# Expert weights in pairs of contraction steps: rows of 22 and 24 KB, and two double ring slots in place of four

## The reference, cut to what matters

```python
affinity = softmax(h @ w_r)                       # 256 tokens, 16 experts
gate, idx = top_k(swapaxes(affinity, 1, 2), 32)   # each expert takes its 32 best tokens
xs = h[idx]                                       # 16 x 32 x 1024
hid = silu(xs @ w_g) * (xs @ w_u)                 # w_g, w_u: 16 x 1024 x 2816
ye = (hid @ w_d) * gate                           # w_d: 16 x 2816 x 1024
out = segment_sum(ye, idx)                        # back to 256 tokens
```

## Time and profile before

| | us |
|---|---|
| runs | 2527.23, 2523.57, 2525.76 |
| median | 2525.76 |
| span of the profiled execution | 2528.1 |
| PE busy | 1933.1 (76%) |
| DVE, ACT, POOL busy | 610.9, 533.0, 585.5 |
| share of the DMA queue of SP, of 16 engines | 74.8% |

### The profile page before, as it was taken

The page is one execution under the profiler, slowest core; times in us unless marked ns, Lnnn a source line. Parts: engine busy times, 40 slices in busy tenths (PEclk is TensorE's granted clock), DMA queues, the critical chain, the costliest instruction groups (busy, mean ns, idle before and its releaser), DMA issues.

```text
span 2528.1 us, 34453 instructions
## 1 busy us (share of the span) xinstructions
PE 1933.1 (76%) x14760; PEld 1173.2 (46%) x14760; DVE 610.9 (24%) x854; ACT 533.0 (21%) x847; POOL 585.5 (23%) x290
## 2 busy tenths in 40 slices
PE   5999887667766666667666676667998989897886
PEld 3786652221121211221112112216888989786776
DVE  4006630000000000000000000014238982235244
ACT  3331221000000000000000000004645434553552
POOL 1435300000000000000000000004626866563562
PEclk7999886665566656665666655667998999997897
DMA  8757489999999999999999999991543546342330
GB/s 338 258 186 288 148 309 400 423 421 426 425 426 425 425 426 426 425 425 426 426 425 426 425 426 425 425 413 62 167 134 125 175 150 194 124 133 84 123 128 17
DMA packets 157966, 760.54 MB, mean 301 GB/s; under 512 B 9751, under 2 KB 101655, under 8 KB 104120
## 3 DMA queue, kind: packets, MB, share of 16 engines
q1 hardware_dynamic: 154216, 754.07, 74.8%
q10 hardware_dynamic: 3664, 5.24, 0.6%
HBM read 756.13 MB, written 3.14 MB: 300 GB/s over the span
## 4 chain that ended last, share of the span: by engine, by line
DMA 44%; PE 40%; DVE 10%; issue 2%; ACT 2%; POOL 1%; SPq 0%; DVEq 0%; ACTq 0%; POOLq 0%
DMA ring<-in_w_exp_down 16%; PE ps L559 15%; DMA ring<-in_w_exp_up 14%; DMA ring<-in_w_exp_gate 13%; PE ps L793 7%; PE ps L553 3%; PE ps L914 2%; PE ps L806 2%; DVE arena L1565 2%; PE ps L513 2%; DVE ff_parts L1566 2%; PE ps L585 2%; DVE ff_parts L1567 1%; PE ps L896 1%; PE ps L679 1%
## 5 line engine op out<-in xcount | busy, mean ns | idle before, releaser
L793 PE MATMUL ps<-ring,arena 128*32 128x352 f32 x4096 | 625.2, 757 | 239.8 <-DMA ring<-in_w_exp_gate 135.5
L1630 POOL TENSOR_TENSOR ring_lo<-ring,w_hi 128x1024 fp32r<-128x1024 f32 x220 | 531.2, 2427 | 588.2 <-ACT w_hi L957 587.9
L559 PE MATMUL ps<-x_parts,w_hi 128*128 128x256 f32 x2688 | 537.5, 296 | 50.5 <-DVE x_parts L1266 40.1
L559 PEld LDWEIGHTS ps<-x_parts,w_hi 128*128 128x128 f32 x2688 | 444.4, 198 | 79.2 <-issue 48.1
L793 PEld LDWEIGHTS ps<-ring,arena 128*32 128x32 f32 x4096 | 147.0, 153 | 704.6 <-DMA ring<-in_w_exp_gate 258.8
L559 PE MATMUL ps<-x_parts,ring_lo 128*128 128x256 f32 x1344 | 391.5, 291 | 0.0
L806 PE MATMUL ps<-ring,arena 128*32 128x256 f32 x2816 | 235.3, 489 | 178.3 <-DMA ring<-in_w_exp_down 131.8
L559 PEld LDWEIGHTS ps<-x_parts,ring_lo 128*128 128x128 f32 x1344 | 267.8, 199 | 0.2 <-issue 0.2
L806 PEld LDWEIGHTS ps<-ring,arena 128*32 128x32 f32 x2816 | 98.8, 135 | 323.1 <-DMA ring<-in_w_exp_down 185.0
L957 ACT ACTIVATE w_hi<-ring 128x1024 fp32r<-128x1024 f32 x220 | 229.8, 1053 | 89.6 <-PE ps L914 50.3
L1477 DVE TENSOR_TENSOR arena<-arena,ps 128x704 f32<-128x704 f32 x16 | 14.2, 887 | 827.8 <-PE ps L793 827.8
(11 more groups left out here) (200 smaller groups left out, 1655.0 us busy)
## 6 DMA issues: line engine op xcount, KB each, us to landing
ring<-in_w_exp_gate SPq DMA_DIRECT2D x128, 1408.0 KB, 10.7
ring<-in_w_exp_up SPq DMA_DIRECT2D x128, 1408.0 KB, 10.9
ring<-in_w_exp_down SPq DMA_DIRECT2D x112, 1536.0 KB, 11.5
ring<-in_w_ada SPq DMA_DIRECT2D x48, 1536.0 KB, 8.7
ring<-in_w_in SPq DMA_DIRECT2D x30, 1536.0 KB, 7.2
ring<-in_w_ff SPq DMA_DIRECT2D x18, 1536.0 KB, 7.1
ring<-in_w_in SPq DMA_DIRECT2D x16, 1024.0 KB, 5.5
ring<-in_w_out SPq DMA_DIRECT2D x8, 1536.0 KB, 7.3
```

What stands on the lines that cost most here:

```text
L559: m = pe.matmul(ps[:, bank, 0:T], w, a, start=(k == 0 and j == 0), stop=(k == KD - 1 and j == 2))
L793: m = pe.matmul(ps[32 * j:32 * j + 32, 2 * (k // 8) + i, 0:FJ // 2], XCUR[:, k % 8, :], ring[:, s, at:at + FJ // 2], start=(k % 8 == 0), s ...
L1630: pool.tensor_tensor(slot(c["u"], KD, c["w"], of=ring_lo)[:, :, at], slot(c["u"], KD, c["w"])[:, :, at], w_hi[:, s % HI, :, :].bitcast(F32 ...
```

## The change

Two contraction steps are loaded together. The four slots are seen as two of 24 KB per partition (`ring_pairs`), with semaphores of their own, `pair_ready` and `pair_used`. An expert has 12 pairs: 4 of gate, 4 of up, 4 of down. A pair waits until the pair that held its slot before is used.

For gate and up, partition p now holds features 8 p to 8 p + 7, so that a pair is one row of 22 KB per partition, the rows 88 KB apart. To match, block c of XS takes every eighth feature: HTOK is read with a step of 8 floats. A pair of down is a row of 24 KB, the last one 16 KB. SP's loop over the experts is written out, the waits of ACT, DVE and POOL count pairs, and POOL's first copy of XCUR stands ahead of its loop. The number of matmuls and their order on PE stay as they are.

```diff
-EXP_UNITS = 24
+EXP_RING = 2
+EXP_PAIRS = 12
+DOWN_C = 6
...
+        pair_ready = [S(f"pair_ready{i}") for i in range(EXP_RING)]
...
+        ring_pairs = ring.rearrange("p (a b) n -> p a (b n)", a=EXP_RING)
...
             def load(u, dst, src):
-                if u >= RING:
+                if exp0 <= u < exp0 + RING:
+                    last = EXPERTS * EXP_PAIRS - EXP_RING + u % RING // (RING // EXP_RING)
+                    sp.wait_ge(S("pair_used"), last + 1)
+                elif u >= RING:
                     sp.wait_ge(S("unit_used"), u - RING + 1)
                 sp.dma_start(dst, src).then_inc(w_ready[u % RING], 16)
...
-            gate = inp["w_exp_gate"].rearrange("a e (k p) f -> (a e) p k f", p=P)
-            up = inp["w_exp_up"].rearrange("a e (k p) f -> (a e) p k f", p=P)
+            gate = inp["w_exp_gate"].rearrange("a e (p k) f -> (a e) p (k f)", p=P)
+            up = inp["w_exp_up"].rearrange("a e (p k) f -> (a e) p (k f)", p=P)
             down = inp["w_exp_down"].rearrange("a e (p c) d -> (a e) p (c d)", p=P)
-            with sp.Fori(0, EXPERTS) as e:
-                for k in range(EXP_UNITS):
-                    sp.wait_ge(S("unit_used"), e * EXP_UNITS + (exp0 + k - RING + 1))
-                    s = (exp0 + k) % RING
-                    if k < 16:
-                        src = (gate if k < 8 else up)[e, :, k % 8, :]
-                        dst = ring[:, s, 0:F_EXP]
+            for e in range(EXPERTS):
+                for q in range(EXP_PAIRS):
+                    n = e * EXP_PAIRS + q
+                    i = n % EXP_RING
+                    if n < EXP_RING:
+                        sp.wait_ge(S("unit_used"),
+                                   1 + max(u for u in range(exp0) if u % RING // (RING // EXP_RING) == i))
                     else:
-                        c0 = 3 * (k - 16)
-                        c1 = min(c0 + 3, FC)
+                        sp.wait_ge(S("pair_used"), n - EXP_RING + 1)
+                    if q < 8:
+                        src = (gate if q < 4 else up)[e, :, 2 * (q % 4) * F_EXP:2 * (q % 4 + 1) * F_EXP]
+                        dst = ring_pairs[:, i, 0:2 * F_EXP]
+                    else:
+                        c0 = DOWN_C * (q - 8)
+                        c1 = min(c0 + DOWN_C, FC)
                         src = down[e, :, c0 * D:c1 * D]
-                        dst = ring[:, s, 0:(c1 - c0) * D]
-                    sp.dma_start(dst, src).then_inc(w_ready[s], 16)
+                        dst = ring_pairs[:, i, 0:(c1 - c0) * D]
+                    sp.dma_start(dst, src).then_inc(pair_ready[i], 16)
...
-                    m = pe.matmul(ps[:, c % 4, :], HTOK[:, t, P * c:P * c + P], SEL[:, t, :, :],
+                    m = pe.matmul(ps[:, c % 4, :], HTOK[:, t, :].rearrange("p (q k) -> p k q", k=KD)[:, c, :],
+                                  SEL[:, t, :, :],
                                   start=(t == 0), stop=(t == NT - 1))
...
+                for q in range(8):
+                    pe.wait_ge(pair_ready[q % EXP_RING], e * (16 * EXP_PAIRS // EXP_RING) + 16 * (q // EXP_RING + 1))
+                    for k in (0, 1):
+                        x = XCUR[:, 2 * (q % 4) + k, :]
+                        for i in range(2):
+                            for j in range(CG):
+                                at = F_EXP * k + FJ * j + FJ // 2 * i
+                                m = pe.matmul(ps[32 * j:32 * j + 32, 2 * (q // 4) + i, 0:FJ // 2], x,
+                                              ring_pairs[:, q % EXP_RING, at:at + FJ // 2],
+                                              start=(q % 4 == 0 and k == 0), stop=(q % 4 == 3 and k == 1),
+                                              skip_group_check=True)
+                    count(m, "pair_used")
...
+                for q in range(8, EXP_PAIRS):
+                    pe.wait_ge(pair_ready[q % EXP_RING], e * (16 * EXP_PAIRS // EXP_RING) + 16 * (q // EXP_RING + 1))
+                    c0 = DOWN_C * (q - 8)
+                    for c in range(c0, min(c0 + DOWN_C, FC)):
...
-            with pool.Fori(0, EXPERTS) as e:
-                pool.wait_ge(S("unit_used"), e * EXP_UNITS + (exp0 - 8))
-                pool.tensor_copy(XCUR, xs[:, :, e, :]).then_inc(S("xcur"), 1)
+            pool.tensor_copy(XCUR, xs[:, :, 0, :]).then_inc(S("xcur"), 1)
+            with pool.Fori(0, EXPERTS - 1) as e:
                 pool.wait_ge(S("scattered"), e + 1)
                 pool.tensor_copy(PGCUR, PGT[:, e, :]).then_inc(S("pgcur"), 1)
+                pool.wait_ge(S("pair_used"), e * EXP_PAIRS + 8)
+                pool.tensor_copy(XCUR, xs[:, :, e + 1, :]).then_inc(S("xcur"), 1)
```

More of the change, by code:

```diff
@@ L201, in build @@
     exp0 = plan.n
-    for _ in range(EXPERTS * EXP_UNITS):
-        plan.unit()
-    assert EXP_UNITS % RING == 0
+    assert EXP_PAIRS % EXP_RING == 0
     in2 = plan.dense(4608, lambda n: ["lat"], [(8, 12), (16, 20)])
@@ L804, in _ @@
                         for j in range(CG):
                             at = D * (c - c0) + T * j
-                            m = pe.matmul(ps[32 * j:32 * j + 32, 4, 0:T], HIDT[:, c, :], ring[:, s, at:at + T],
+                            m = pe.matmul(ps[32 * j:32 * j + 32, 4, 0:T], HIDT[:, c, :],
+                                          ring_pairs[:, q % EXP_RING, at:at + T],
                                           start=(c == 0), stop=(c == FC - 1), skip_group_check=True)
-                    count(m, "unit_used")
+                    count(m, "pair_used")
@@ L1096, in _ @@
             with act.Fori(0, EXPERTS) as e:
-                act.wait_ge(S("unit_used"), e * EXP_UNITS + (exp0 + 8))
+                act.wait_ge(S("pair_used"), e * EXP_PAIRS + 4)
                 act.wait_ge(S("hid_done"), e + 1)
                 act.activation(SIL, ps[:, 0:2, 0:FJ // 2], ACT.Silu).then_inc(S("sil"), 1)
-                act.wait_ge(S("unit_used"), e * EXP_UNITS + (exp0 + EXP_UNITS))
+                act.wait_ge(S("pair_used"), e * EXP_PAIRS + EXP_PAIRS)
                 act.wait_ge(S("scattered"), e + 1)
@@ L1475, in _ @@
                 waits("sil", e + 1)
-                waits("unit_used", e * EXP_UNITS + (exp0 + 16))
+                waits("pair_used", e * EXP_PAIRS + 8)
                 tt(HID.rearrange("p (i f) -> p i f", i=2), SIL, ps[:, 2:4, 0:FJ // 2], ALU.mult).then_inc(S("hid_done"), 1)
@@ L1664, in _ @@
             xs = XS.rearrange("p k (e s) -> p k e s", e=EXPERTS)
[L1665 to L1667 removed]
+            pool.tensor_copy(XCUR, xs[:, :, 0, :]).then_inc(S("xcur"), 1)
+            with pool.Fori(0, EXPERTS - 1) as e:
                 pool.wait_ge(S("scattered"), e + 1)
                 pool.tensor_copy(PGCUR, PGT[:, e, :]).then_inc(S("pgcur"), 1)
+                pool.wait_ge(S("pair_used"), e * EXP_PAIRS + 8)
+                pool.tensor_copy(XCUR, xs[:, :, e + 1, :]).then_inc(S("xcur"), 1)
+            pool.wait_ge(S("scattered"), EXPERTS)
+            pool.tensor_copy(PGCUR, PGT[:, EXPERTS - 1, :]).then_inc(S("pgcur"), 1)
             low_parts(in3[0][0]["items"][0]["s"] + 2)
```

## The result

The changed kernel takes 2672.22 us in the median of four runs (2662.83 to 2680.37) against 2526.49 before: a ratio of 1.0579, 95% interval 1.0555 to 1.0602, 146 us slower. I had forecast slower by 39 us, 2565, with an upper end of 2612. The direction was right, the size was not, and the range missed.

What follows compares the result with a forecast made beforehand. The expert stage was taken as bound by its DMA stream. Per expert -0.9 + 2.2 + 1.0 = +2.3 us, +37 for 16, plus 2 for the end, gave +39 us: 2565, range 2514 to 2612.

Steps and rivals of the forecast that it cites:

- The long rows: Expert weight loads: half as many rows per engine, 9 ns saved for each, -0.9 us per expert, bounds 0 and -1.8.
- the first rival: Expert stream stays full and only the longer rows' gain is left: 2514 us, or 2500 with 9 ns doubled; chance 0.15.
- The transfers of 6.70 and 7.31 us: Expert loads: a gate or up pair transfers in 6.70 us, a down pair with 24 KB rows in 7.31 us.
- the layout at nothing: Gate and up loads: rows now 88 KB apart cost nothing, as down loads already read that way at the same rate.
- the strided weight load hidden: Token gather: HTOK read with a step of 8 floats in 32 weight loads, taken as 0, 6 us if exposed.
- PE's bursts of 3.5 to 4.9 us: Gate and up: time PE uses a pair, with its clock expected to rise late in many bursts.
- the clock that rises in part of them: Gate and up: PE's clock expected to rise from 1.2 GHz late in many bursts and fall in the gap.
- the tail: End of the experts: the last down pair lands whole, leaving PE 16 steps where 4 were left: +2 us.
- the start: First pair waits for the two oldest adaln units in place of one, in a still busy stream: 0.
- Two double slots in place of four: Gate and up: a pair costs the larger of its transfer and half its slot's cycle; +2.2 us per expert, 0 to 3.6.
- The seams: Between stages of an expert: up to down idles 0.5 to 1.2 us, taken as 1.0; to the next expert, covered.
- all at the lower clock: Rival: PE at 1.2 GHz throughout, 2611 us, or near 2680 with 3.3 us for start-up and landing; chance 0.15.

Runs made afterwards that it cites:

- experiments 7 and 9: 7: changed kernel with a third double slot, 2512.89 us; 9: that kernel with loads issued later by an added wait, 2571.11 and 2654.67 us.
- experiment 7: Changed kernel with a third double slot, 2512.89 us; also the kernel before with six single slots in place of four, 2526.3 us.
- experiment 5: One load at a time, issued after PE has used the load before: kernel before 4541.0 us, changed kernel 3830.24 us.
- three double slots: Changed kernel with a third double slot in 24 KB of the arena: 2512.89 us, ratio 0.9946 to the kernel before.
- light PE: Changed kernel with half of PE's gate, up and down steps left out and no wait for the transpose: 2573.52 us.
- half of PE's use: Changed kernel with the second of two contraction steps of each gate and up pair left out of the matmuls: 2594.79 us.
- half wait: Changed kernel with a third double slot, where SP issues pair n only when PE is half through pair n - 2: 2571.11 us.
- full wait: Changed kernel with a third double slot, where SP issues pair n only when PE is through pair n - 2: 2654.67 us.

## Why the prediction was wrong in size

**Right, point by point.** The direction and its mechanism, two slots that are issued too late, stand (experiments 7 and 9). The long rows: 0.9 us per expert were forecast, and with the stream full the period goes from 81.3 to 80.4 (experiment 7). They are worth their 14 us, and with a third slot they arrive as the first rival had it, 2514; the change as made does not let them. The transfers of 6.70 and 7.31 us, the layout at nothing, the strided weight load hidden, PE's bursts of 3.5 to 4.9 us in gate and up (mean 4.2; twelve of 127 are under 3), the clock that rises in part of them, the tail (1.93 us for the last 16 steps) and the start were right too. The Trainium skill, "SBUF — State Buffer", section "Door 1: The DMA port swizzle", has a penalty for each access that crosses to a new 16-byte line. The trace agrees that the 32-byte step costs the weight load something, 314 ns in place of 190; the kernel's time does not show it. The Trainium skill, "DMA: Bandwidth & Descriptors", section "Anatomy of one DMA", gives about 2.0 us as the fixed cost, mostly completion, and gives it for loads that GpSimd issues, which the prediction left out; the loads here are issued by SP. For these the traces show another size, 2.4 to 2.5 us, and only 0.33 us of it behind the last row (experiment 5). By 2.0 the forecast would have been further off.

**The step that failed** is the price of a pair in "Two double slots in place of four": "a pair costs the larger of its transfer and half of that cycle", with the 2.6 us of a load alone put into the cycle. The 2.6 were right and the maximum was not. The forecast gave gate and up 2.2 us per expert, with 3.6 as the upper bound; measured are 5.3 us, beside another 1.5 on the first gate pair. The table puts the interval of gate or up pairs (6.70 us when nothing is lost) beside what is queued, taken as the time from an issue to the end of the transfer ahead of it on the slowest engine, for the pairs in mid-stream:

| kernel | queued at the issue, us | interval, us |
|---|---|---|
| three double slots | 8.6 to 8.9 | 6.70 |
| light PE | 3.7 to 3.9 | 6.8 to 7.0 |
| half of PE's use | 3.6 to 3.9 | 6.7 to 6.9 |
| half wait | 4.0 to 4.4 | 6.9 to 7.0 |
| full wait | 2.2 to 3.2 | 7.1 to 7.6 |
| the change | 2.5 to 3.1 | 7.6 to 7.7 |

By my cycle 2.2 us in the queue were enough. They are not: at 2.5 to 3 a pair loses 0.9 us, and even at 3.8 some 0.1 to 0.2. One place does not follow the table: the second gate pair of an expert has 6.2 us queued with the light PE and 6.6 with the half wait and still loses 0.15 and 0.2, behind a first pair that came 1.6 to 1.9 us late.

**Why a load in a half-dry queue comes later than the maximum says.** In mid-stream a pair of the change lands 11.0 us after its issue. Right behind the pair ahead (3.3 us to its landing, and 6.7) it would be 10.0, alone 9.1. The traces tell this much of the rest. The 16 engines of a load do not land together: in the change 1.5 to 1.9 us lie between first and last from the fourth pair of an expert on. A load is issued only after PE has used one of which the last engine has landed, so the engines that are ahead have that much less in their queue and run dry first. Engines out of step cost nothing by themselves: they lie 1.9 us apart with three double slots and 2.7 in the kernel before, both at full rate. They cost where the queue is short: with half of PE's use they lie 0.8 us apart and a pair loses 0.1 us, with the light PE 1.7 us apart and a pair loses 0.2, with as much queued.

Taken for each engine by itself, four kernels with short queues tell the same. The table has the share of cases in which an engine ran dry before its next row, by what it had left when the next load was issued (the first three experts left out; the packets do not name their engine, but each engine's rows follow each other without a gap and close with a 4-byte packet):

| left on the engine at the issue, us | the change | light PE | half wait | full wait |
|---|---|---|---|---|
| under 1 | 95% | 89% | 87% | 94% |
| 1 to 2 | 34% | 44% | 44% | 32% |
| 2 to 3.5 | 16% | 8% | 8% | 18% |
| 3.5 and more | 1% | 1% | 0% | 0% |

With three double slots no engine has less than 3.7 us left, and none runs dry. Why an engine with 1 to 3.5 us left runs dry at times, when the first row of a load alone begins 0.96 us after the issue, stays open; in the kernel before, in full stream, 318 such cases (11 KB rows) saw none. An engine that has run dry takes 1.3 us in the mean for its first row of 22 KB (1.4 where every load starts dry, experiment 5), against 0.84 in mid-stream. About half of the extra row time of the change lies in such first rows, the rest in rows of engines that had not run dry: the mean of all is 0.89. In the kernel with three double slots it is 0.84 with hardly one row over. This is the other half of the loss, the one that the DMA share hides: 0.95 busy at 90% of the rate. One engine's delay becomes the landing of the whole, and so the next issue of all. What stretches the rows of the others is not shown. No run forced engines apart or together.

**The seams** were the second term that was mis-sized. "The seam to the next expert is covered by the 6.7 us of the gate pair in transfer" overlooked that this gate pair itself is issued behind the short last pair of 4.9 us; it loses 1.5 us in the change and 1.9 with the light PE. And for down I had taken PE's use of a pair at the higher clock, 3.0 us; it was mostly 4.3 to 5.4 (1086.80 and 1095.05 in the timeline of the change), so its 24 KB pairs were issued late too and lost time. Down and its seam cost 3.3 us where 1.0 was given.

Sum per expert: -0.9 (as forecast), +5.3 for gate and up (2.2), +1.5 for the first gate pair (0), +3.3 for down (1.0): 9.2, and 16 of them make 147 us, where 146 were measured in the medians. The closeness is partly luck: these terms are means over experts 4 to 16, the first ones lose less, and the profiled executions differ by 141.

The range failed for one reason: its upper end was worked out with the same maximum. The case "all at the lower clock" with 2.6 us gave 2611, and the same case with 3.3 us, from the load that took 7.0 us beside another one, gave near 2680, which I left out of the range. The measured 2672 lies next to it, but that case does not describe the run: the granted clock of the stage rose to 0.72 and most bursts of gate and up were shorter than 4.9 us. No row showed a load in a half-dry queue of this kind, so the upper bound should have lain beyond both.

## What to carry to other kernels

When loads are merged into fewer and larger ones in the same memory, the question is not only whether a slot's cycle fits into the transfers of the others, but how many microseconds of transfer are queued at the moment of each issue, on the slowest engine and on the one that is furthest ahead. Here, for pairs, 6.5 us and more at every issue kept the stream at its full rate, 3.8 us lost up to 3% and 2.5 to 3 us some 13% of a pair (the kernel before, with 11 KB rows, stayed at its full rate with 5.4 us at the least), while the arithmetic with the latency of a load alone said that 2.2 would do. Longer rows are a real but small gain (1.2% for 22 KB against 11 KB), worth taking only with a slot more of memory.

## What the runs showed of the hardware that I had not expected

- A load alone needs 2.4 to 2.5 us beside its transfer for rows of 11 and of 22 KB alike (5.9, 6.1, 9.1, 9.7 us from issue to landing): 0.96 us to the first row, 0.33 us from the last row to the landing, and 1.2 us in late beginnings and longer first rows.
- An engine with 3.5 us or more of its own rows left at the next issue hardly ever ran dry, one with less than 1 us left in some nine of ten cases.
- DMA share and rate part company: 0.99 busy at 410 GB/s, 0.95 at 382, 1.00 at 430. The share alone says nothing of rows that are stretched.
- Weight loads of 128 columns read with a step of 8 floats take 314 ns in place of 190.
